# Hybrid decoder step on Trainium2: four experts packed on three tiles of 128 places

## The reference, cut to what matters

```python
D_MODEL, EXPERT_DIM = 1024, 256
gsel = argmax(xt @ w_router_group + b_router_group)
vals, eidx = top_k(le_sel, 2)          # the two experts inside the group
hg = silu(xt @ w_expert_gate[e]) * (xt @ w_expert_up[e])
out += (hg * weight) @ w_expert_down[e]
y = layer_norm(ALPHA * h + out)
```

## Time and profile before

| what | us |
|---|---|
| median of 3 executions | 1569.9 |
| lowest and highest of them | 1568.22, 1572.11 |
| the profiled execution | 1573.19 |
| its span, first to last instruction | 1571.7 |
| PE busy in it | 1445.2 (92%) |
| VectorE, ScalarE, GpSimd busy | 724.6, 297.6, 255.3 |

### The profile page before, as it was taken

How to read it: one execution, slowest core, us unless ns; L and a number is a source line. 1 busy time by engine, 2 the same in 40 slices (tenths; PEclk the granted TensorE clock), 3 DMA queues, 4 the chain that set the end, 5 groups by cost and what they waited for, 6 DMA issues and landing times. The chain is left out here.

```text
span 1571.7 us, 17708 instructions
## 1 busy us (share of the span) xinstructions
PE 1445.2 (92%) x5707; PEld 783.7 (50%) x5707; DVE 724.6 (46%) x1639; ACT 297.6 (19%) x656; POOL 255.3 (16%) x308
## 2 busy tenths in 40 slices
PE   7999999799999999898979898999399999999974
PEld 2444444344566666565756564555244444444421
DVE  0201023788888889954548445555411111111134
ACT  0100122221221111113554200000111111111123
POOL 3131000133310000101341000111211111111112
PEclk9999999799999999998999899999699999999998
DMA  9221001300121111102331295000189998999658
GB/s 314 64 63 34 15 15 68 128 0 1 43 103 62 70 61 60 70 19 60 91 89 55 79 371 219 28 27 27 60 338 353 336 353 335 354 337 350 254 124 220
DMA packets 74507, 221.90 MB, mean 141 GB/s; under 512 B 16738, under 2 KB 42338, under 8 KB 65098
## 3 DMA queue, kind: packets, MB, share of 16 engines
q1 hardware_dynamic: 58170, 184.64, 33.4%
q0 software_dynamic: 14992, 35.90, 6.5%
q10 hardware_dynamic: 1280, 0.53, 0.2%
HBM read 190.56 MB, written 38.84 MB: 146 GB/s over the span
## 5 line engine op out<-in xcount | busy, mean ns | idle before, releaser
L1786 PE MATMUL main_ps_experts<-w_gate_up,main_e_rowsT 128*128 128x512 f32 x512 | 227.8, 598 | 1.2 <-DVE main_e_rowsT L1891 1.2
L234 PE MATMUL ps_front<-front,x_all 128*128 128x512 f32 (+1 forms) x448 | 183.8, 566 | 1.7 <-ACT wi L364 1.7
L906 DVE TENSOR_SCALAR_CACHE_REDUCE front<-score,bound 128x384 bf16<-128x384 f32 (+2 forms) x198 | 174.2, 942 | 19.2 <-DVE bound L932 18.9
L1786 PEld LDWEIGHTS main_ps_experts<-w_gate_up,main_e_rowsT 128*128 128x128 f32 x512 | 95.8, 192 | 110.6 <-issue 110.6
L234 PEld LDWEIGHTS ps_front<-front,x_all 128*128 128x128 f32 x448 | 84.4, 193 | 93.9 <-issue 83.4
L1519 PE MATMUL ps_merge<-w_o,mergedT 128*128 128x512 f32 x256 | 113.6, 602 | 3.0 <-DVE h_rows L1650 3.0
L733 PE MATMUL ps_gate<-x_all,w_gate 128*128 128x344 f32 x384 | 115.9, 461 | 0.0
L1813 PE MATMUL main_ps_experts<-w_down,main_hiddenT 128*128 128x512 f32 x256 | 115.3, 593 | 0.5 <-ACT main_hiddenT L1848 0.5
L1896 DVE TENSOR_TENSOR main_hidden<-main_hidden,main_ps_experts 128x256 f32<-128x256 f32 x32 | 13.5, 421 | 221.2 <-ACT main_hidden L1843 221.2
L733 PE MATMUL ps_gate<-x_all,front 128*128 128x344 f32 x384 | 113.2, 453 | 0.0
L733 PEld LDWEIGHTS ps_gate<-x_all,w_gate 128*128 128x128 f32 x384 | 74.3, 194 | 38.8 <-issue 2.3
(11 more groups left out here) (296 smaller groups left out, 1787.4 us busy)
## 6 DMA issues: line engine op xcount, KB each, us to landing
w_gate_up<-in_w_gate_up SPq DMA_DIRECT2D x32, 2048.0 KB, 8.3
w_down<-in_w_down SPq DMA_DIRECT2D x32, 1024.0 KB, 11.2
w_gate_up<-pair_out SPq DMA_DIRECT2D x16, 512.0 KB, 18.0
front<-in_w_qkvi SPq DMA_DIRECT2D x8, 930.0 KB, 19.1
w_gate<-in_w_gate SPq DMA_DIRECT2D x4, 1280.0 KB, 5.9
front<-in_w_gate SPq DMA_DIRECT2D x4, 1280.0 KB, 5.9
h_rows<-in_x_rows SPq DMA_DIRECT2D x9, 512.0 KB, 6.0
h<-h_rows SPq DMA_DIRECT2D x9, 512.0 KB
```

The source lines that it names most:

```text
L234: mm = nc.tensor.matmul(ps[:, g % 2, 0:c1 - c0], x_all[:, k, t * P:(t + 1) * P], w[:, k, c0:c1], start=(k == 0), stop=(k == KC - 1))
L906: V.tensor_scalar(waste[0:n, at - width:at], s, column(bound, g), None, compare, ALU.add, accum_out=column(number, g)).then_inc(taken, 1)
L1786: mm = nc.tensor.matmul(ps[:, GU, :], rowsT[j][:, k, :], w_gu[jw][:, k, :], start=(k == 0), stop=(k == KC - 1))
```

## The change

Four experts (a quad) are packed on three tiles (packs) of 128 places. Each expert has 96 places (`SHARE`), in a row: expert 0 on places 0 to 95 of pack 0, expert 1 on 96 to 127 of pack 0 and 0 to 63 of pack 1, expert 2 on 64 to 127 of pack 1 and 0 to 31 of pack 2, expert 3 on 32 to 127 of pack 2. There are 24 packs for 32 tiles. Each matmul of `make_hidden` and `make_result` becomes two or three (`PARTS`): for each stretch of places of 32 or 64, one matmul that holds those places as its columns of the array and streams the whole 512 columns of that expert's weights, into its part of the PSUM partitions. Gate-up and down weights get semaphores of their own, and SP loads them when gate-up and down of the packs that use them are done; experts 2 and 3 are loaded at once. The loops over experts are unrolled. `place` computes the new address: rank divided by 96, the lane in the quad, the pack by comparison with 128 and 256. The rest of the list is worked through if an expert has more than 96 tokens. Some small buffers move into the spent attnT.

```diff
@@ -1345,6 +1345,10 @@
 F = 256
 W_BUFS = 4
 W_AHEAD = 2
+SHARE = 96
+QUAD = 4
+PACKS = N_EXPERTS // QUAD * 3
+PARTS = (((0, 64, 0), (64, 96, 0), (96, 128, 1)), ((0, 64, 1), (64, 128, 2)), ((0, 32, 2), (32, 64, 3), (64, 128, 3)))
 SLOTS = TOK * N_EXPERTS
 NOWHERE = float(1 << 20)
 ROUTER = N_GROUPS + N_EXPERTS
@@ place @@
             def place(i):
 
                 t = tiles[i]
                 dve.wait_ge(ranked, i + 1)
-                step(V.scalar_tensor_tensor(marked, ps[:, 3 + i % 2, 0:N_EXPERTS], float(N_EXPERTS), expert[:],
-                                            ALU.mult, ALU.add))
+                ranks = ps[:, 3 + i % 2, 0:N_EXPERTS]
+                step(V.tensor_scalar(share, ranks, 683.0, None, ALU.mult))
+                step(V.tensor_scalar(share, share, 16, None, ALU.logical_shift_right))
+                step(V.scalar_tensor_tensor(lin, share, -float(SHARE), ranks, ALU.mult, ALU.add), wait=False)
+                step(V.scalar_tensor_tensor(address, share, float(P * PACKS), column[:], ALU.mult, ALU.add))
+                step(V.tensor_tensor(lin, lin, lane[:], ALU.add))
+                step(V.tensor_scalar(wrap, lin, float(P), None, ALU.is_ge))
+                step(V.scalar_tensor_tensor(wrap, lin, float(2 * P), wrap, ALU.is_ge, ALU.add), wait=False)
+                step(V.scalar_tensor_tensor(address, lin, float(PACKS), address, ALU.mult, ALU.add))
+                step(V.scalar_tensor_tensor(marked, wrap, 1.0 - P * PACKS, address, ALU.mult, ALU.add))
                 for which in range(2):
-                    step(V.tensor_tensor(waste, choice[which][i % 2][:], marked, ALU.mult))
-                    step(V.tensor_reduce(slot[:, which:which + 1], waste, AX.X, ALU.add))
+                    step(V.scalar_tensor_tensor(waste, choice[which][i % 2], 1.0, marked, ALU.mult, ALU.mult,
+                                                accum_out=slot[:, which:which + 1]))
                 V.tensor_tensor(slot_out[:, :, t], slot[:], away[:, t:t + 1].to_broadcast([P, 2]),
                                 ALU.add).then_inc(slots_ready, 1)
 
@@ -1721,39 +1737,50 @@
 
         @block.sync
         def _(sp):
-            def load(e, j):
-                sp.dma_start(w_gu[j][:], ins["w_gate_up"][bass.ds(e, 1)]).then_inc(w_in[j], 16)
-                sp.dma_start(w_dn[j][:], ins["w_down"][bass.ds(e, 1)]).then_inc(w_in[j], 16)
-
-            lists = scratch["list_of"].rearrange("(c p e) o -> c p (e o)", p=P, e=N_EXPERTS)
-            sp.dma_start(entries[:], lists[bass.ds(chunk, 1)]).then_inc(list_in, 16)
-            for j in range(loaded, W_BUFS):
-                if j >= 2:
-
-                    sp.wait_ge(rows_in[j - 2], 16)
-                load(j, j)
+            def load_gate_up(e):
+                sp.dma_start(w_gu[e % W_BUFS][:], ins["w_gate_up"][e]).then_inc(w_gu_in[e % W_BUFS], 16)
+
+            def load_down(e):
+                sp.dma_start(w_dn[e % W_BUFS][:], ins["w_down"][e]).then_inc(w_dn_in[e % W_BUFS], 16)
+
+            lists = scratch["list_of"].rearrange("(c p n) o -> c p (n o)", p=P, n=PACKS)
+            sp.dma_start(entries, lists[bass.ds(chunk, 1)]).then_inc(list_in, 16)
+            for e in range(loaded, W_BUFS):
+                load_gate_up(e)
+                load_down(e)
             if loaded:
                 for to, name in ((keep["ln2"][:, 0, :], "ln2_g"), (keep["ln2"][:, 1, :], "ln2_b"),
                                  (keep["minus_half2"][:], "minus_half")):
                     src = ins[name]
                     sp.dma_start(to, src.to_broadcast([P, src.shape[1]]) if src.shape[0] == 1 else src
                                  ).then_inc(keep["f_const_in"], 16)
-            with sp.Fori(1, N_EXPERTS // W_BUFS) as i:
-                for j in range(W_BUFS):
-
-                    sp.wait_ge(down, (i * W_BUFS + (j - W_BUFS)) * 2 + 2)
-                    load(i * W_BUFS + j, j)
+            for g in range(1, N_EXPERTS // QUAD):
+                e, s = g * QUAD, 3 * (g - 1)
+                sp.wait_ge(gate_up, s + 1)
+                load_gate_up(e)
+                sp.wait_ge(gate_up, s + 2)
+                load_gate_up(e + 1)
+                sp.wait_ge(down, 2 * s + 2)
+                load_down(e)
+                sp.wait_ge(gate_up, s + 3)
+                load_gate_up(e + 2)
+                load_gate_up(e + 3)
+                sp.wait_ge(down, 2 * s + 4)
+                load_down(e + 1)
+                sp.wait_ge(down, 2 * s + 6)
+                load_down(e + 2)
+                load_down(e + 3)
             if loaded:
-                sp.wait_ge(down, 2 * N_EXPERTS)
+                sp.wait_ge(down, 2 * PACKS)
                 for j in range(2):
-                    sp.wait_ge(stored[j], 16 * N_EXPERTS // 2)
+                    sp.wait_ge(stored[j], 16 * PACKS // 2)
                 last.sync(sp)
 
         @block.gpsimd
         def _(pool):
             pool.wait_ge(tokens_ready, 1)
-            for e in range(N_EXPERTS + 3):
-                if e < N_EXPERTS:
+            for e in range(PACKS + 3):
+                if e < PACKS:
                     if e >= 2:
 
                         pool.wait_ge(rows_turned, 2 * (e - 2) + 2)
@@ -1770,20 +1797,26 @@
                                             in_=result[r % 2][:], in_offset=None,
                                             bounds_check=2 * TOK - 1, oob_is_err=False).then_inc(stored[r % 2], 16)
             for j in range(2):
-                pool.wait_ge(stored[j], 16 * N_EXPERTS // 2)
+                pool.wait_ge(stored[j], 16 * PACKS // 2)
             if loaded:
                 last.gpsimd(pool)
 
         @block.tensor
         def _(pe):
-            def make_hidden(e, jw):
-                j = jw % 2
-                pe.wait_ge(w_in[jw], (e - jw) * (32 // W_BUFS) + 32)
-                pe.wait_ge(rowsT_act, e + 2)
-                pe.wait_ge(rowsT_dve, e + 2)
-                pe.wait_ge(hid, e + 1)
+            def wait_for(loads, s):
+                for b in ((0, 1), (2,), (3,))[s % 3]:
+                    pe.wait_ge(loads[b], 16 * (s // 3 + 1))
+
+            def make_hidden(s, _):
+                j = s % 2
+                wait_for(w_gu_in, s)
+                pe.wait_ge(rowsT_act, s + 2)
+                pe.wait_ge(rowsT_dve, s + 2)
+                pe.wait_ge(hid, s + 1)
                 for k in range(KC):
-                    mm = nc.tensor.matmul(ps[:, GU, :], rowsT[j][:, k, :], w_gu[jw][:, k, :], start=(k == 0), stop=(k == KC - 1))
+                    for c0, c1, b in PARTS[s % 3]:
+                        mm = nc.tensor.matmul(ps[c0:c1, GU, :], rowsT[j][:, k, c0:c1], w_gu[b][:, k, :],
+                                              start=(k == 0), stop=(k == KC - 1))
                 mm.then_inc(gate_up, 1)
 
             def turn_rows(e, jw):
@@ -1807,16 +1840,18 @@
             def make_result(e, jw):
                 j = jw % 2
                 pe.wait_ge(hidT_read, e + 2)
+                wait_for(w_dn_in, e)
                 for c, read in enumerate((down_act, down_dve)):
                     pe.wait_ge(read, e + 1)
                     for k in range(F // P):
-                        mm = nc.tensor.matmul(ps[:, 4 + 2 * j + c, :], hiddenT[j][:, k, :], w_dn[jw][:, k, c * 512:(c + 1) * 512],
-                                              start=(k == 0), stop=(k == F // P - 1))
+                        for c0, c1, b in PARTS[e % 3]:
+                            mm = nc.tensor.matmul(ps[c0:c1, 4 + 2 * j + c, :], hiddenT[j][:, k, c0:c1],
+                                                  w_dn[b][:, k, c * 512:(c + 1) * 512], start=(k == 0), stop=(k == F // P - 1))
                     mm.then_inc(down, 1)
 
             if loaded:
                 nc.tensor.matmul(counts, keep["ones"][:], keep["chosen"][:, TILES, :], start=True, stop=True).then_inc(counted, 1)
-            staggered(pe, N_EXPERTS, [(2, turn_hidden), (1, make_hidden), (0, turn_rows), (2, make_result)], W_BUFS)
+            staggered(pe, PACKS, [(2, turn_hidden), (1, make_hidden), (0, turn_rows), (2, make_result)], 2, loop=False)
             if loaded:
                 pe.wait_ge(weighed, 1)
                 last.tensor_swap(pe)
@@ -2175,8 +2211,8 @@
         experts(nc, ins, outs, keep, scratch, 0, loaded=W_AHEAD, tag="main")
 
         longest = nc.values_load(keep["most"][:], min_val=0, max_val=TOK)
-        with nc.If(longest > P):
-            with nc.Fori(1, (longest + (P - 1)) // P) as chunk:
+        with nc.If(longest > SHARE):
+            with nc.Fori(1, (longest + (SHARE - 1)) // SHARE) as chunk:
                 experts(nc, ins, outs, keep, scratch, chunk, loaded=0, tag="rest")
             finish_again(nc, outs, keep, scratch)
 
```

More of the change, by code:

```diff
@@ L1380, in merge_and_route @@
         empty = h[:, TILES - 1, 0:SLOTS // P].bitcast(U32)
-        fall, expert = sb("fall", [P, N_EXPERTS]), sb("expert", [P, N_EXPERTS])
+        fall, lane, column = (sb(n, [P, N_EXPERTS]) for n in ("fall", "lane", "column"))
```

(27 more changed lines are left out.)

21 lines of the change are left out of this document (11 added, 10 removed).

## The result

The changed kernel takes 1710.1 us (median of 4 executions, 1701.4 to 1712.0) against 1569.6 us: ratio 1.088, 95% interval [1.084, 1.092], slower by some 140 us. The forecast was 1720. The profiled execution has a span of 1710.6 us, 138.9 more than before.

What follows compares the result with a forecast made beforehand. It took the expert stage to be bound by PE, with DMA close behind. Products +140, start of stage +5.8 and placing +3.5 gave 149.5 us, so 1720 us for the median; range 1515 to 1755, this case's own 1695 to 1755.

Steps and rivals of the forecast that it cites:

- this case: Mixed packs: groups of 64 and 32 run serially with drains; 1720 us, range 1695 to 1755, chance 0.57.
- The products: Expert stage: a mixed k (groups of 64 and 32) costs 2.0 us, a quad 63.1 against 45.6, +140 us.
- Full overlap, the rival on the other side: Mixed packs: unequal groups run side by side, DMA bounds at 39 us per quad; 1524 us, 1505 to 1550, chance 0.30.
- Gaps, but overlap: Mixed packs: size changes delay weights but streams overlap, 1.14 us per k; 1554 us, chance 0.08.
- The second pass: Expert stage: a choice beyond 96 places opens 24 more packs, over 2000 us; chance 0.01.
- The start of the stage: First gather: weights issued ahead delay it from 4.1 to 9.9 us, +5.8 us, bounds 0 and 7.5.
- Placing: place() on VectorE: more operations, 2.8 us each, +1.5 per tile; +3.5 us on the path, bounds 2 and 5.

Runs made afterwards that it cites:

- experiment 1: Changed kernel with each group of 64 in the first and third packs cut into two of 32: 1488.3 us, ratio 0.957 to the kernel before.
- experiment 4: Changed kernel with one 32-group product in the first and third packs computed only at k = 0: 1692.9 us, ratio 1.086 to the kernel before.
- experiment 3: Changed kernel with the order of products within k reversed at every odd k: 1678.4 us, ratio 1.078 to the kernel before.
- experiment 7: Changed kernel with all products on 64 first, then all on 32, in each mixed pack: ratio 1.066 to the kernel before.
- experiment 5: Changed kernel with loads of experts 2 and 3 waiting for the first two gathers again: ratio 1.087 to the kernel before.
- experiment 8: Kernel before the change, with loads of experts 2 and 3 issued without waiting for the first two gathers: ratio 1.0027 to the kernel before.
- experiment 6: Changed kernel with all packs on groups of 32 and the old wait ahead of experts 2 and 3: ratio 0.952 to the kernel before.
- experiment 2: Changed kernel with all packs, the middle one too, on groups of 32: 1484.2 us, ratio 0.952 to the kernel before.

## Why the prediction was right

The 1710.1 us lie in this case's own range, 1695 to 1755 (its terms add up to some 1750 at the top), and the case had the largest chance, 0.57.

**The products.** Right in mechanism and size. Forecast 2.0 us per mixed k, measured 1.99; 63.1 us per quad, measured 62.42; +140 for eight quads, measured 8 x (62.42 - 45.6) = +134.6. The two halves of the sum were tested apart: a whole turn for each size (experiments 1 and 4), and a price for every change, which experiments 3 and 7 put at 0.134 us as the mean of both directions, where the sum took 0.135 and 0.15. The 5 us too many come from small excesses in every term: 23.83 us of products per mixed pack for 24.0, 1.39 of transposes (1.02 + 0.37) for 1.5, 12.0 per middle pack for 12.1. By the Trainium skill ("TensorEngine Tiling (Array Packing)", Key Properties) changing the tiling mode drains the engine; the loads held up for 0.81 us at every change agree, and they show it for sizes that lie on different columns.

**Full overlap, the rival on the other side.** Fell as stated: equal groups overlap, unequal ones don't. But what it said of a kernel without that loss could be read in experiment 1, and there one step was wrong. It priced DMA at 379 to 414 GB/s and took 39 us a quad. The stage held 419 GB/s over 150 us, and the quad took 35.9, close to the 36.4 that it had for PE. With the ratio of experiment 1 the kernel would take 0.957 x 1569.6 = 1502 us, below the 1524 and just below the rival's range. The Trainium skill ("HBM Reference", Specifications (TRN2)) has a core that streams alone at about 425 GB/s, which agrees; the 358 GB/s weighed in the prediction is its figure for a core whose neighbour streams too.

**Gaps, but overlap** fell with the changed kernel's own trace: it had 1.14 us for a mixed k, measured are 1.99, and the groups of 32 start 1.00 us after the group of 64, when both its passes have been streamed (1203.95 against 1202.94). Experiment 3 agrees: with half of the changes gone, only 0.13 us went with each. **The second pass** was not entered: there are 24 gathers and 24 packs of products.

**The start of the stage.** Forecast +5.8, measured 9.2 - 4.1 = +5.1 at the transposes; experiment 5 shows 4.8 of it gone there with the wait back (6.1 for the stage), experiment 8 5.1 coming without the wait, so the cause is the loads ahead of the gather.

**Placing.** Forecast 2.8 us for the last place(), measured 1121.00 to 1123.39, 2.4. Timeline of VectorE after, answering to the earlier trace rows:

```profile
1121.00 0.19 DVE L1638 TENSOR_SCALAR attnT<-ps_merge 128x32 int32<-128x32 f32 x1 [1.15 <-PE ps_merge L1556]
...
1121.45 0.19 DVE L1640 SCALAR_TENSOR_TENSOR attnT<-attnT,ps_merge 128x32 f32<-128x32 int32 x1
1121.55 0.18 DVE L1641 SCALAR_TENSOR_TENSOR attnT<-attnT,column 128x32 f32<-128x32 int32 x1
...
1123.23 0.16 DVE L1650 TENSOR_TENSOR slot_out<-slot,away 128x2 uint32<-128x2 f32 x1
```

Nine steps at 0.22 was too much: the two without a wait behind them let the next start after 0.10 and 0.11 us. The rank that answers to the one at 1113.29 of the earlier trace rows, in the timeline of PE after:

```profile
1111.98 0.63 PE L1555 MATMUL ps_merge<-attnT,earlier 128*128 128x32 f32 x2 [0.60 <-DVE chosen L1631]
```

From there to the first gather it is 1132.96 - 1111.98 = 20.98 us against 1131.55 - 1113.29 = 18.26: +2.7, forecast +3.5. Of it 1.1 is the last place() itself (2.39 us for 1.28), where the sum had 1.5 each time. No run took place() alone.

**What the spans hide.** The gather is issued only 1.4 us later than before, since that rank came 1.3 us sooner. This is not the change's: in experiments 1 to 7, whose code ahead of it is the same, the first gather is issued anywhere from 1114.4 to 1120.0 us. The account of the span is then 514.3 - 375.4 = 138.9 for the stage (134.6 for the quads, 5.1 for the first gather, and 0.8 less that no term names), + 2.7 for placing, - 1.3 for what came ahead, - 1.4 for the last stage: 138.9. The last stage isn't the change's either: from the last down product to the end it takes 63.2 to 64.8 us in the ten traces, 63.3 after the change and 64.8 before. So of the 10.6 us by which the forecast of 149.5 was too high, 7 lie in its three terms, all a little too large, and most of the rest in stretches that vary from run to run.

## What to carry to other kernels

In this kernel (float32, 512 streamed columns) several products on column groups ran in nearly the time of one when all groups that alternate had one size (0.88 us per k for 0.86), and took a full extra turn when they hadn't (1.99): cut every group to the smallest size needed. Here one table turned 8.8% slower into 4.8% faster than before. Look for the cost in the times of the weight loads. Bulk loads issued ahead of the small transfer that a stage starts with delayed it by 5 us; where DMA was near its limit anyway (experiment 6), a third of what the old order gained was given back.

## What the runs showed that was not expected

- Size, not place, decides: a group of 64 and a group of 32 on other columns, without a dependence between them, ran one after the other wherever they alternated, while four groups of 32 with up to two experts' weights ran at once. The price of a change was the same, 0.13 us, whether 1, 8 or 15 of them lay in a product.
- One core held 419 to 421 GB/s for 150 us while PE was busy for over 99% of it (experiments 1 and 2).
- The stage's first gate-up product ran at a mean granted clock of 0.91 in experiment 5 and 0.85 in the changed kernel, worth 1.2 us. The standstill ahead of it was shorter there (6.3 us in place of 11.3), but between the kernel before and experiment 8 (6.15 and 11.50) the clock didn't differ (0.72 and 0.73), so the cause is open.
